# A snapshot copy moved on ScalarE, relu and square of the MLP moved to VectorE, and the last pair of a group split by unit, in a two-layer streaming encoder on one core

## The chip, the cores and the metric

One Trainium2 chip, one of its cores. A time is the device time in microseconds (us) of the whole kernel, one launch. The core has five engines that run their own instruction streams and meet at semaphores: TensorE (PE, with its weight loads shown as PEld), VectorE (DVE), ScalarE (ACT), GpSimd (POOL) and SyncE (SP, which issues the DMAs).

## The reference

Two layers over 512 prompt frames and 32 sample frames, which the kernel handles together as 544 columns. Each layer has a normalised projection, retention, gated linear attention and band attention in parallel, an output projection, and an MLP. The change is in the MLP:

```python
def channel_mix(h, n2, w_up_l, w_down_l):
    u = rmsnorm(h, n2) @ w_up_l                              # 1024 -> 4096
    return (jnp.square(jax.nn.relu(u)) @ w_down_l).astype(h.dtype)   # 4096 -> 1024
...
    for l in range(DEPTH):                                   # DEPTH = 2
        hp = hp + merge_heads(...)
        hp = hp + channel_mix(hp, norm2_w[l], w_up[l], w_down[l])
```

The RMS factor of the norm is not applied ahead of the up projection; the kernel scales after the down projection with its square (r2), which relu and square allow.

## The kernel before

All matrix products are made in fp32 with three passes: every operand is split into a high part (fp32r, a rounded copy made by ScalarE) and a rest (made by VectorE, original minus high part), and TensorE multiplies high by high, high by rest and rest by high. So each weight block and each activation passes through ScalarE (`whi`, `zhi`, ...) and then VectorE (`wlo`, `zlo`, ...) before TensorE can take it.

The MLP of a layer has four groups of 1024 hidden units (`GROUPS`). A group has eight units of 128 hidden rows, taken two at a time as four **pairs**, and then eight down units (`down` to `down + 7`). A pair is not multiplied out as it stands, but with seven products of quarter matrices (a fast scheme of the Strassen kind), numbered 6, 7, 5, 1, 2, 3, 4; each is 12 matmuls of 128x128 by 272 columns. TensorE's order in the steady state is `product(6, j)`, `(7, j)`, `(5, j)`, then `(1, j+1)`, `(2, j+1)`, then `(3, j)`, `(4, j)`. For the last pair of a group the first down unit stands between products 5, 3 and 4. The four weight combinations of a pair are `whi[0]/wlo[0]` (r0, also product 1 of the next pair), `R1h/R1l` (r1, products 6 and 7), `whi[1]/wlo[1]` (r2, product 5 and others) and `R3h/R3l` (r3, product 4).

Products accumulate in PSUM in part over each other, so ScalarE takes snapshots between them: `snap_s1` (L795 to L801) copies product 1 out of its bank before product 6 may add to it, `snap_u2` copies after product 6, before product 5, and `snap_x` after product 5. VectorE then adds snapshots and PSUM into the four quarters of `cb`, the pair's two units of 544 columns: `add_c11`, `add_c22`, `add_c21`; ScalarE writes c12 (`read_c12`). `post` (L828) on ScalarE then does relu in place, square in place and the high copy `zhi`, each over both units (1088 columns), and `rest_z` (L1503) on VectorE makes `zlo`. Down units wait for `z_lo` of the pair whose rows they use.

The order on every engine is written out by hand, in program order. Engines are in-order, so an instruction that waits holds all behind it. What matters here:
- At the MLP's start TensorE runs products 1 and 2 of the first pair (three quarters of 2, then 6 in part). `open_pair` (L1996) makes product 6 wait for `r1_lo` and `s1_read`, product 5 for `r2_lo` and `u2_read`, product 1 of the next pair for `r0_lo`.
- ScalarE at that point finishes the new activations of the MLP: `new_x` (L729) for the eighth tile, `hi_r2(0)`, `new_square(7)`, and then the loop over groups begins with `snap_s1(0)` (L906).
- VectorE in a pair: `add_c21(j-1)`, `lo_r2(j)`, `add_c11(j)`, `lo_r0(j+1)` (for the last pair `rest(down)`), `lo_r3(j)`, the sums of weights of the next pair, `add_c22(j)`, `rest_z(j-1)`, `lo_r1(j+1)`.
- After a group's last pair, in the first group of a layer only, VectorE works out r2 (an affine step and two reciprocals, L1583 and L1588), then in each group `rest(down+2)` and `scaled(0)` (L1526), which reads the first down unit out of PSUM. TensorE's `begin(down+2)` waits for both.
- GpSimd sums the squares and reduces them over partitions once a layer at the MLP's start, and adds each scaled down unit to `h`.

Of the kernel before, what the change touches and what calls it, by code (L numbers as in the profile page):

```python
# [9 lines left out]
KC = D // P  # L10
# [82 lines left out]
for _steps in (DVE_STEPS, ACT_STEPS):  # L93
# [16 lines left out]
    pvs_dve=4, gate_act=8, gate_dve=8, cat_dve=4, cat_hi=4, cat_lo=4, z_hi=16, z_lo=16,  # L110
# [59 lines left out]
def dve_x(name, kc):  # L170
    return len(DVE_X) * kc + DVE_X[name]

# [25 lines left out]
def hybrid_encoder(nc, x, wu, w_low, a2, small, bias, bias_s, st_ret, st_gla, ck, cv,  # L198
# [3 lines left out]
    with ctx:  # L202
# [115 lines left out]
        def sem(name):  # L318
# [25 lines left out]
            "split_act", "split_dve",  # L344
# [8 lines left out]
        with nc.Block() as block:  # L353
# [168 lines left out]
            def _(act):  # L522
# [10 lines left out]
                for layer in range(L):  # L533
# [192 lines left out]
                    def new_x(m):  # L726
# [13 lines left out]
                        else:  # L740
                            nc.scalar.activation(Xh[:, 1:3, kc, :], h[:, t, :].rearrange("p (a b) -> p a b", a=2), ACT.Copy,
                                                 scale=w).then_inc(sems["split_act"], 1)
                            act.wait_ge(sems["split_dve"], nth("split_dve", dve_x("t4_sum", kc)))
# [75 lines left out]
                    def read_c12(j):  # L819
# [3 lines left out]
                        if pair >= 2:  # L823
                            act.wait_ge(sems["z_lo"], pair - 1)
# [3 lines left out]
                    def post(j):  # L828

                        pair, q = up(j)[0], j % QUADS  # L830
                        act.wait_ge(sems["c12"], pair + 1)
                        act.wait_ge(sems["c21"], pair + 1)
                        link(nc.scalar.activation(cb[j % 2][:, :, :], cb[j % 2][:, :, :], ACT.Relu))
                        link(nc.scalar.activation(cb[j % 2][:, :, :], cb[j % 2][:, :, :], ACT.Square))
                        nc.scalar.activation(zhi[:, 2 * q:2 * q + 2, :], cb[j % 2][:, :, :], ACT.Copy).then_inc(sems["z_hi"], 1)

                    def next_x(m):
# [5 lines left out]
                        act.wait_ge(sems["z_lo"], nth("z_lo", PAIRS))  # L843
# [3 lines left out]
                    def last_squares(m):  # L847

                        act.wait_ge(sems["sq_used"], nth("sq_used", GROUPS * KC + m + 1))
                        act.wait_ge(sems["z_lo"], nth("z_lo", PAIRS))  # L850
# [53 lines left out]
                    for g in range(GROUPS):  # L904
                        j0, down = QUADS * g, UP + g * N_MLP + KC
                        snap_s1(j0)  # L906
# [20 lines left out]
                        post(j0 + QUADS - 1)  # L927
# [33 lines left out]
            def _(dve):  # L961
# [7 lines left out]
                for layer in range(L):  # L969
# [506 lines left out]
                    def add_c11(j):  # L1476
# [6 lines left out]
                        else:  # L1483
                            dve.wait_ge(sems["z_lo"], pair - 1)
# [17 lines left out]

                    def rest_z(j):  # L1503

                        pair, q = up(j)[0], j % QUADS
                        dve.wait_ge(sems["z_hi"], pair + 1)
# [46 lines left out]
                    for g in range(GROUPS):  # L1553
                        j0, down = QUADS * g, UP + g * N_MLP + KC
                        for j in range(j0, j0 + QUADS):
                            more = j + 1 < j0 + QUADS
                            if j > j0:
                                add_c21(j - 1)
                                lo_r2(j)
                            add_c11(j)  # L1560
# [19 lines left out]
                        rest_z(j0 + QUADS - 1)  # L1580
# [64 lines left out]
            def _(pe):  # L1645
# [6 lines left out]
                for layer in range(L):  # L1652
# [568 lines left out]
```

## Time and profile before

| | |
|---|---|
| three runs | 1408.93, 1405.13, 1407.30 us; median 1407.3 us |
| profiled execution, its own time | 1408.74 us |
| its span, first to last instruction | 1407.0 us |
| mean granted TensorE clock | 0.985 of full |
| TensorE matmul busy | 1352.0 us (96%) |
| VectorE busy | 939.8 us (67%) |
| ScalarE busy | 650.6 us (46%) |
| GpSimd busy | 155.4 us (11%) |
| DMA | 127.83 MB, 91 GB/s on average |

An engine's busy share is an average over the span. Matmuls overlap in the pipeline: one is listed at 0.29 us, but one starts every 0.126 us at the full clock. A bracket at the end of a timeline row tells how long the engine sat idle before that instruction, and what released it as far as the trace shows; "issue" means that nothing in the trace was found.

### The profile page before, as it was taken

The numbers are of one execution on the slowest core, as the hardware profiler recorded it, in microseconds if no ns is written. First come the engines' busy times: TensorE is split into PE (matmuls) and PEld (weight loads), VectorE is DVE, ScalarE is ACT, GpSimd is POOL, SyncE is SP. The second block draws the span as 40 slices with busy tenths as digits, with TensorE's granted clock in tenths as the row PEclk, the third lists the DMA queues.
The fourth block names the chain that finished last, engine by engine and source line by source line (L and its number), as shares of the span: only waits on it lengthen the run. The fifth ranks groups of instructions, "written<-read, shape, count | busy, mean of one in ns | idle before, by whom it ended". The sixth has DMA issues, their size and how long they took to land. (4 is left out here: it accounts for less than half of the span.)

```text
span 1407.0 us, 28738 instructions
## 1 busy us (share of the span) xinstructions
PE 1352.0 (96%) x12206; PEld 1307.8 (93%) x12206; DVE 939.8 (67%) x1464; ACT 650.6 (46%) x1043; POOL 155.4 (11%) x107
## 2 busy tenths in 40 slices
PE   9999999999999999999999999999999999999996
PEld 8899889899999999999998999889999999999996
DVE  6797766787657366475758967767774664746734
ACT  4423656655526337255333236565562362542731
POOL 0100000021120120210302000001201102012012
PEclk9999999999999999999999999999999999999998
DMA  5213333222322223222221223432222232232211
GB/s 218 76 57 109 96 111 103 76 90 75 104 92 77 91 90 105 81 85 93 91 75 47 67 84 119 132 97 76 76 75 98 84 106 90 76 105 90 87 64 64
DMA packets 50639, 127.83 MB, mean 91 GB/s; under 512 B 8400, under 2 KB 17744, under 8 KB 50512
## 3 DMA queue, kind: packets, MB, share of 16 engines
q1 hardware_dynamic: 50224, 125.44, 27.0%
q8 instruction: 97, 1.59, 0.5%
q10 hardware_dynamic: 288, 0.55, 0.1%
q14 instruction: 30, 0.25, 0.1%
HBM read 118.77 MB, written 7.21 MB: 90 GB/s over the span
## 5 line engine op out<-in xcount | busy, mean ns | idle before, releaser
L1666 PE MATMUL PS<-zhi,whi 128*128 128x272 f32 x1280 | 370.9, 290 | 15.4 <-DVE sq L1531 14.9
L1666 PE MATMUL PS<-zhi,wlo 128*128 128x272 f32 x1280 | 371.5, 290 | 0.0
L1666 PE MATMUL PS<-zlo,whi 128*128 128x272 f32 x1280 | 369.5, 289 | 0.0
L979 DVE TENSOR_TENSOR wlo<-raw,whi 128x1024 fp32r<-128x1024 f32 x136 | 169.0, 1243 | 162.4 <-ACT whi L548 161.5
L548 ACT ACTIVATE whi<-raw 128x1024 fp32r<-128x1024 f32 x136 | 143.4, 1056 | 286.8 <-PE PS L1666 281.3
L1666 PE MATMUL PS<-xhi,whi 128*128 128x272 f32 x896 | 270.2, 302 | 5.4 <-DVE xlo L984 2.9
L1666 PE MATMUL PS<-xhi,wlo 128*128 128x272 f32 x896 | 260.2, 290 | 0.0
L1666 PE MATMUL PS<-xlo,whi 128*128 128x272 f32 x896 | 259.5, 290 | 0.0
L1666 PEld LDWEIGHTS PS<-zhi,whi 128*128 128x128 f32 x1280 | 242.3, 189 | 17.4 <-DVE wlo L979 17.4
L1666 PEld LDWEIGHTS PS<-zlo,whi 128*128 128x128 f32 x1280 | 242.5, 189 | 0.0
L1666 PEld LDWEIGHTS PS<-zhi,wlo 128*128 128x128 f32 x1280 | 241.9, 189 | 0.0
L1666 PEld LDWEIGHTS PS<-xhi,whi 128*128 128x128 f32 x896 | 170.3, 190 | 17.1 <-issue 8.4
L1666 PEld LDWEIGHTS PS<-xlo,whi 128*128 128x128 f32 x896 | 170.6, 190 | 0.2
L513 POOL TENSOR_TENSOR h<-h,sq 128x544 f32<-128x544 f32 x62 | 102.1, 1650 | 620.8 <-DVE sq L1531 620.8
L1666 PEld LDWEIGHTS PS<-xhi,wlo 128*128 128x128 f32 x896 | 170.2, 190 | 0.0
L1666 PE MATMUL PS<-Xh,wlo 128*128 128x272 f32 x384 | 111.5, 290 | 0.0
L1666 PE MATMUL PS<-Xh,whi 128*128 128x272 f32 x384 | 111.4, 290 | 0.0
L1666 PE MATMUL PS<-Xl,whi 128*128 128x272 f32 x384 | 110.7, 288 | 0.0
L1666 PE MATMUL PS<-Th,R1h 128*128 128x272 f32 x256 | 76.5, 299 | 6.1 <-issue 6.1
L1666 PE MATMUL PS<-Th,R1l 128*128 128x272 f32 x256 | 76.1, 297 | 0.0
L1666 PE MATMUL PS<-Tl,R1h 128*128 128x272 f32 x256 | 75.7, 296 | 0.0
L1666 PEld LDWEIGHTS PS<-Xl,whi 128*128 128x128 f32 x384 | 72.8, 189 | 0.0
(282 smaller groups left out, 2445.7 us busy)
## 6 DMA issues: line engine op xcount, KB each, us to landing
raw<-in_wu SPq DMA_DIRECT2D x199, 512.0 KB, 3.5
Bh<-in_bias SPq DMA_DIRECT2D x16, 256.0 KB, 4.2
h<-in_x SPq DMA_DIRECT2D x8, 272.0 KB, 6.6
out_k_t<-att_k SPq DMA_DIRECT2D x8, 272.0 KB, 4.4
out_y_t<-y SPq DMA_DIRECT2D x8, 272.0 KB, 2.7
kct<-in_ck SPq DMA_DIRECT2D x8, 256.0 KB, 3.3
cvb<-in_cv SPq DMA_DIRECT2D x8, 256.0 KB, 3.9
out_v_p<-vtk SPq DMA_DIRECT2D x8, 256.0 KB, 2.2
```

The lines of the kernel that those rows point to most:

```text
L513: nc.gpsimd.tensor_tensor(h[:, m, :], h[:, m, :], sq[m % 2][:, :], ALU.add) \
L548: nc.scalar.activation(whi[n % SPL][:, :], raw[n % RAW][:, :], ACT.Copy).then_inc(sems["w_hi"], 1)
L979: nc.vector.tensor_tensor(wlo[n % SPL][:, :], raw[n % RAW][:, :], f32(whi[n % SPL][:, :]), ALU.subtract).then_inc(sems["w_lo"], 1)
L1666: return nc.tensor.matmul(out, lhsT, rhs, start=start, stop=stop, skip_group_check=True)
```

## The change

1. `snap_s1(0)`, the copy of product 1 of the layer's first pair, is issued inside `new_x` for the last tile, behind the high copy `Xh` and ahead of the copy `Th`, and no longer at the head of the first group. Other groups keep it where it was.
2. `post` on ScalarE keeps the high copy alone. Relu and square of a pair are one operation on VectorE, `relu_square`: `scalar_tensor_tensor` computes max(c, 0) * c over 1088 columns, in place. It stands between `lo_r2(j)` and `add_c11(j)`, for pair `j-1`. A new semaphore `row_squared` tells ScalarE.
3. The last pair of a group is split by its two units. Unit 0 (c11 and c12) stays on ScalarE (relu, square, high copy, 544 columns each); unit 1 gets its max-and-multiply on VectorE, its high copy on ScalarE; two rests of 544 columns on VectorE. Down products 6 and 7 wait each for their own unit. The counts of `z_hi` and `z_lo` go from 16 to 20 a layer.

TensorE's stream of instructions is the same in both kernels.

```diff
@@ new_x, last tile, ScalarE
                             nc.scalar.activation(Xh[:, 1:3, kc, :], h[:, t, :].rearrange("p (a b) -> p a b", a=2), ACT.Copy,
                                                  scale=w).then_inc(sems["split_act"], 1)
+                            if m == KC - 1:
+                                snap_s1(0)
                             act.wait_ge(sems["split_dve"], nth("split_dve", dve_x("t4_sum", kc)))
...
@@ ScalarE
                     def post(j):
                         pair, q = up(j)[0], j % QUADS
+                        act.wait_ge(sems["row_squared"], pair + 1)
+                        nc.scalar.activation(zhi[:, 2 * q:2 * q + 2, :], cb[j % 2][:, :, :], ACT.Copy).then_inc(sems["z_hi"], 1)
+
+                    def last_post(j):
+                        pair, c = up(j)[0], cb[j % 2]
+                        act.wait_ge(sems["c11"], pair + 1)
                         act.wait_ge(sems["c12"], pair + 1)
-                        act.wait_ge(sems["c21"], pair + 1)
-                        link(nc.scalar.activation(cb[j % 2][:, :, :], cb[j % 2][:, :, :], ACT.Relu))
-                        link(nc.scalar.activation(cb[j % 2][:, :, :], cb[j % 2][:, :, :], ACT.Square))
-                        nc.scalar.activation(zhi[:, 2 * q:2 * q + 2, :], cb[j % 2][:, :, :], ACT.Copy).then_inc(sems["z_hi"], 1)
+                        link(nc.scalar.activation(c[:, 0, :], c[:, 0, :], ACT.Relu))
+                        link(nc.scalar.activation(c[:, 0, :], c[:, 0, :], ACT.Square))
+                        nc.scalar.activation(zhi[:, KC - 2, :], c[:, 0, :], ACT.Copy).then_inc(sems["z_hi"], 1)
+                        act.wait_ge(sems["row_squared"], pair + 1)
+                        nc.scalar.activation(zhi[:, KC - 1, :], c[:, 1, :], ACT.Copy).then_inc(sems["z_hi"], 1)
...
@@ group loop, ScalarE
-                        snap_s1(j0)
+                        if g:
+                            snap_s1(j0)
...
-                        post(j0 + QUADS - 1)
+                        last_post(j0 + QUADS - 1)
...
@@ VectorE
+                    def relu_square(j):
+                        pair, c = up(j)[0], cb[j % 2]
+                        dve.wait_ge(sems["c12"], pair + 1)
+                        dve.wait_ge(sems["c21"], pair + 1)
+                        nc.vector.scalar_tensor_tensor(c[:, :, :], c[:, :, :], 0.0, c[:, :, :], ALU.max, ALU.mult) \
+                            .then_inc(sems["row_squared"], 1)
...
+                    def last_rest_z(j):
+                        pair, c = up(j)[0], cb[j % 2]
+                        dve.wait_ge(sems["c21"], pair + 1)
+                        nc.vector.scalar_tensor_tensor(c[:, 1, :], c[:, 1, :], 0.0, c[:, 1, :], ALU.max, ALU.mult) \
+                            .then_inc(sems["row_squared"], 1)
+                        for row in range(2):
+                            k = KC - 2 + row
+                            dve.wait_ge(sems["z_hi"], z_done(pair, row))
+                            nc.vector.tensor_tensor(zlo[:, k, :], c[:, row, :], f32(zhi[:, k, :]), ALU.subtract) \
+                                .then_inc(sems["z_lo"], 1)
...
@@ pair loop, VectorE
                                 add_c21(j - 1)
                                 lo_r2(j)
+                                relu_square(j - 1)
                             add_c11(j)
...
@@ down units, TensorE
-                            pe.wait_ge(sems["z_lo"], nth("z_lo", j0 + kc // 2 + 1))
+                            pe.wait_ge(sems["z_lo"], z_done(layer * PAIRS + j0 + kc // 2, kc % 2))
```

What the engines' streams look like at three places, before and then changed. First ScalarE at the start of the first layer's MLP. `Xh` and `Th` are high parts of activations, `whi1` is the weight high part r2 for product 5, `sq1` a square for the norm, `s1_sb` the snapshot of product 1, `whi0` the weight part r0 of the next pair, `u2_sb0` the snapshot that product 5 waits for.

```order
L741 ACTIVATE Xh_153<-h_57,sm_81 128x2x272 [waits unit_read]
L744 ACTIVATE Th_151<-tt1_164 128x3x272 [waits split_dve]
L783 ACTIVATE whi1_54<-Sx_159 128x1024 [waits unit_done,s4_ready]
L750 ACTIVATE sq1_65<-h_57 128x544 [waits sq_used]
L800 ACTIVATE s1_sb_165<-PS 128x272 [waits prod]
L765 ACTIVATE whi0_53<-raw2_51 128x1024 [waits prod,w_in2]
L808 ACTIVATE u2_sb0_167<-PS 128x272 [waits prod]
```

```order
L747 ACTIVATE Xh_153<-h_57,sm_81 128x2x272 [waits unit_read]
L808 ACTIVATE s1_sb_165<-PS 128x272 [waits prod]
L752 ACTIVATE Th_151<-tt1_164 128x3x272 [waits split_dve]
L791 ACTIVATE whi1_54<-Sx_159 128x1024 [waits unit_done,s4_ready]
L758 ACTIVATE sq1_65<-h_57 128x544 [waits sq_used]
L773 ACTIVATE whi0_53<-raw2_51 128x1024 [waits prod,w_in2]
L816 ACTIVATE u2_sb0_167<-PS 128x272 [waits prod]
```

`s1_sb` went from behind three instructions to ahead of them; the copy `whi0` and the snapshot `u2_sb0` follow `sq1` directly now.

Second VectorE in the middle of a group, pair 2 of the first group: `wlo1` is the rest for product 5, `cb` the pair's result, `wlo0` the rest for product 1 of the next pair.

```order
L1500 TENSOR_TENSOR cb1_161<-PS,u2_sb1_168 128x272 [waits u2_read,prod]
L1437 TENSOR_TENSOR wlo1_56<-Sx_159,whi1_54 128x1024 [waits r2_hi]
L1485 TENSOR_TENSOR cb0_160<-PS,s1_sb_165 128x272 [waits z_lo,s1_read,prod]
L1437 TENSOR_TENSOR wlo0_55<-raw2_51,whi0_53 128x1024 [waits r0_hi]
L1437 TENSOR_TENSOR R3l_158<-raw1_50,R3h_157 128x512 [waits r3_hi]
L1459 TENSOR_TENSOR Sx_159<-raw3_52 128x512 [waits r1_lo,r2_lo,w_in3,w_in2]
```

```order
L1517 TENSOR_TENSOR cb1_161<-PS,u2_sb1_168 128x272 [waits u2_read,prod]
L1454 TENSOR_TENSOR wlo1_56<-Sx_159,whi1_54 128x1024 [waits r2_hi]
L1525 SCALAR_TENSOR_TENSOR cb1_161<-cb1_161 128x1088 [waits c21,c12]
L1502 TENSOR_TENSOR cb0_160<-PS,s1_sb_165 128x272 [waits z_lo,s1_read,prod]
L1454 TENSOR_TENSOR wlo0_55<-raw2_51,whi0_53 128x1024 [waits r0_hi]
L1454 TENSOR_TENSOR R3l_158<-raw1_50,R3h_157 128x512 [waits r3_hi]
L1476 TENSOR_TENSOR Sx_159<-raw3_52 128x512 [waits r1_lo,r2_lo,w_in3,w_in2]
```

One more operation of 1088 columns stands ahead of `wlo0`, `R3l` and all behind them. In the last pair of a group `wlo0` at this place is the rest of the first down unit.

Third VectorE behind the last pair of the first group: `zlo` is the pair's rest, `r2` the scale of the down units, `wlo0` the rest of the third down unit, `sq0` the read of the first one.

```order
L1500 TENSOR_TENSOR cb1_161<-PS,u2_sb1_168 128x272 [waits u2_read,prod]
L1507 TENSOR_TENSOR zlo_61<-cb1_161,zhi_60 128x1088 [waits z_hi]
L1583 TENSOR_SCALAR r2_63<-rstd_62 128x544 [waits ss_all]
L1588 RECIPROCAL r2_63<-r2_63 128x272 [waits r2_steps] x2
L979 TENSOR_TENSOR wlo0_55<-raw2_51,whi0_53 128x1024 [waits w_hi,r2_steps]
L1531 TENSOR_TENSOR sq0_64<-PS,r2_63 128x544 [waits sq_used,unit_done]
```

```order
L1517 TENSOR_TENSOR cb1_161<-PS,u2_sb1_168 128x272 [waits u2_read,prod]
L1539 SCALAR_TENSOR_TENSOR cb1_161<-cb1_161 128x544 [waits c21]
L1544 TENSOR_TENSOR zlo_61<-cb1_161,zhi_60 128x544 [waits z_hi] x2
L1621 TENSOR_SCALAR r2_63<-rstd_62 128x544 [waits ss_all]
L1626 RECIPROCAL r2_63<-r2_63 128x272 [waits r2_steps] x2
L996 TENSOR_TENSOR wlo0_55<-raw2_51,whi0_53 128x1024 [waits w_hi,r2_steps]
L1568 TENSOR_TENSOR sq0_64<-PS,r2_63 128x544 [waits sq_used,unit_done]
```

The rest of 1088 columns became a max-and-multiply and two rests, 544 columns each; what stands behind keeps its order.

## Rows read from the trace of the kernel before

**Rows 1.** Waits of TensorE, whole span: us in total, times, longest.
```profile
PE PS L1666 <- DVE sq L1531: 14.9, 8, 2.4
PE PS L1666 <- issue: 6.1, 2, 3.0
```

**Rows 2.** TensorE's timeline: start us, us, engine, line, operation, [idle before].
```profile
321.90 0.29 PE L1666 MATMUL PS<-Xh,wlo 128*128 128x272 f32 x1
325.23 0.56 PE L1666 MATMUL PS<-Th,R1h 128*128 128x272 f32 x1 [3.04 <-issue]
...
331.54 0.36 PE L1666 MATMUL PS<-Th,whi 128*128 128x272 f32 x1
```

**Rows 3.** ScalarE's timeline at the start of the first layer's MLP.
```profile
320.47 0.75 ACT L741 ACTIVATE Xh<-h,sm 128x544 fp32r<-128x544 f32 x1 [0.59 <-DVE h L1383]
...
324.21 0.64 ACT L750 ACTIVATE sq<-h 128x544 f32<-128x544 f32 x1
324.76 0.38 ACT L800 ACTIVATE s_sb<-PS 128x272 f32<-128x272 f32 x1
328.38 1.06 ACT L765 ACTIVATE whi<-raw 128x1024 fp32r<-128x1024 f32 x1 [3.25 <-PE PS L1666]
331.05 0.40 ACT L808 ACTIVATE u_sb<-PS 128x272 f32<-128x272 f32 x1 [1.60 <-PE PS L1666]
```

**Rows 4.** Stretches: us, busy (instructions) PE, PEld, DVE, ACT, POOL; granted clock; DMA.
```profile
324.50:331.20 6.70, 5.97 (x26) 6.00 (x27) 3.23 (x4) 1.85 (x4) 1.83 (x1) 0.50 0.00 0
...
382.50:385.80 3.30, 3.16 (x14) 3.19 (x15) 1.76 (x2) 0.00 (x0) 3.21 (x2) 0.50 0.65 185
```

**Rows 5.** VectorE's timeline in pair 2 of the first group.
```profile
350.00 0.44 DVE L1500 TENSOR_TENSOR cb<-PS,u_sb 128x272 f32<-128x272 f32 x1 [1.71 <-PE PS L1666]
...
351.84 1.21 DVE L1437 TENSOR_TENSOR wlo<-raw,whi 128x1024 fp32r<-128x1024 f32 x1
...
356.48 1.28 DVE L1507 TENSOR_TENSOR zlo<-cb,zhi 128x1088 fp32r<-128x1088 f32 x1
357.68 1.22 DVE L1437 TENSOR_TENSOR R1l<-Sx,R1h 128x1024 fp32r<-128x1024 f32 x1
360.61 0.44 DVE L1500 TENSOR_TENSOR cb<-PS,u_sb 128x272 f32<-128x272 f32 x1 [1.71 <-PE PS L1666]
```

**Rows 6.** TensorE's weight loads, the first one of product 1 of pair 3.
```profile
354.22 0.19 PEld L1666 LDWEIGHTS PS<-Xh,whi 128*128 128x128 f32 x1
```

**Rows 7.** VectorE, TensorE and its weight load at the second group's third down unit.
```profile
475.84 0.71 DVE L1531 TENSOR_TENSOR sq<-PS,r 128x544 f32<-128x544 f32 x1
...
476.67 0.19 PEld L1666 LDWEIGHTS PS<-zhi,whi 128*128 128x128 f32 x1 [1.88 <-DVE wlo L979]
476.70 0.36 PE L1666 MATMUL PS<-zhi,whi 128*128 128x272 f32 x1 [1.68 <-DVE sq L1531]
```

**Rows 8.** VectorE by form: count, busy us, mean ns, idle before.
```profile
L1351 DVE TENSOR_TENSOR G<-G,sq 128x544 f32<-128x544 f32 x8 | 5.8, 725 | 1.4 <-DVE G L1345 0.5 <-ACT sq L868 0.4
...
L1342 DVE SCALAR_TENSOR_TENSOR sq<-G,sq 128x544 f32<-128x544 f32 x8 | 5.8, 722 | 3.1 <-ACT sq L864 3.1
```

**Rows 9.** GpSimd's reduction at the start of the MLP.
```profile
332.51 3.43 POOL L507 PARTITION_ALL_REDUCE rstd<-ssum  x1 [5.75 <-issue]
```

**Rows 10.** VectorE beside that reduction.
```profile
334.12 1.32 DVE L1473 TENSOR_TENSOR Sx<-raw,Sx 128x512 f32<-128x512 f32 x1
```

**Rows 11.** End of the first group, ScalarE.
```profile
368.48 1.05 ACT L548 ACTIVATE whi<-raw 128x1024 fp32r<-128x1024 f32 x1
```

**Rows 12.** End of the first group, VectorE.
```profile
371.21 0.44 DVE L1500 TENSOR_TENSOR cb<-PS,u_sb 128x272 f32<-128x272 f32 x1 [0.42 <-PE PS L1666]
375.18 1.29 DVE L1507 TENSOR_TENSOR zlo<-cb,zhi 128x1088 fp32r<-128x1088 f32 x1 [3.53 <-ACT zhi L835]
...
380.64 1.22 DVE L979 TENSOR_TENSOR wlo<-raw,whi 128x1024 fp32r<-128x1024 f32 x1
```

**Rows 13.** End of the first group, TensorE.
```profile
382.64 0.56 PE L1666 MATMUL PS<-zhi,whi 128*128 128x272 f32 x1 [2.42 <-DVE sq L1531]
```

More of the change, by code:

```diff
@@ L109 @@
     norm_s=4, pe_turn=8, turned=24, pe_turn_s=4, turned_s=4, pe_pv=4, pv_act=4, pv_dve=4, pe_pv_s=4, pvs_act=4,
-    pvs_dve=4, gate_act=8, gate_dve=8, cat_dve=4, cat_hi=4, cat_lo=4, z_hi=16, z_lo=16,
+    pvs_dve=4, gate_act=8, gate_dve=8, cat_dve=4, cat_hi=4, cat_lo=4, z_hi=20, z_lo=20,
     split_act=20, split_dve=32,
@@ L171, in dve_x, with z_done @@
     return len(DVE_X) * kc + DVE_X[name]
+def z_done(pair, row=1):
+    group, q = divmod(pair, QUADS)
+    return (QUADS + 1) * group + q + (1 if q < QUADS - 1 else 1 + row)
 BANK_A, BANK_B, BANK_C = (4, 5), (2, 6), (3, 7)
@@ L343, in hybrid_encoder @@
             "gate_act", "gate_dve", "cat_dve", "cat_hi", "cat_lo", "z_hi", "z_lo", "out_dma", "stored0", "stored1", "dve_link", "act_link",
-            "split_act", "split_dve",
+            "split_act", "split_dve", "row_squared",
             "s_steps", "s4_ready", "r0_hi", "r0_lo", "r1_hi", "r1_lo", "r2_hi", "r2_lo", "r3_hi", "r3_lo", "prod",
@@ L823, in read_c12 @@
                         if pair >= 2:
-                            act.wait_ge(sems["z_lo"], pair - 1)
+                            act.wait_ge(sems["z_lo"], z_done(pair - 2))
                         nc.scalar.activation(cb[j % 2][:, 0, HT:T], PS[:, BANK_A[j % 2], 0:HT], ACT.Copy) \
@@ L842, in next_x @@
                             act.wait_ge(last_added, 2 * (layer + 1))
-                        act.wait_ge(sems["z_lo"], nth("z_lo", PAIRS))
+                        act.wait_ge(sems["z_lo"], nth("z_lo", z_done(PAIRS - 1)))
                         xhi_tile(m, w0 + NSM)
@@ L849, in last_squares @@
                         act.wait_ge(sems["sq_used"], nth("sq_used", GROUPS * KC + m + 1))
-                        act.wait_ge(sems["z_lo"], nth("z_lo", PAIRS))
+                        act.wait_ge(sems["z_lo"], nth("z_lo", z_done(PAIRS - 1)))
                         squares(m, L)
@@ L1483, in add_c11 @@
                         else:
-                            dve.wait_ge(sems["z_lo"], pair - 1)
+                            dve.wait_ge(sems["z_lo"], z_done(pair - 2))
                         nc.vector.tensor_tensor(cb[j % 2][:, 0, 0:HT], PS[:, BANK_C[j % 2], 0:HT], s1_sb[:, :], ALU.add) \
@@ L1501, in add_c21 @@
                             .then_inc(sems["c21"], 1)
+                    def relu_square(j):
[4 more added lines that the diff above has]
+                            .then_inc(sems["row_squared"], 1)
                     def rest_z(j):
                         pair, q = up(j)[0], j % QUADS
-                        dve.wait_ge(sems["z_hi"], pair + 1)
+                        dve.wait_ge(sems["z_hi"], z_done(pair))
                         nc.vector.tensor_tensor(zlo[:, 2 * q:2 * q + 2, :], cb[j % 2][:, :, :], f32(zhi[:, 2 * q:2 * q + 2, :]),
                                                 ALU.subtract).then_inc(sems["z_lo"], 1)
+                    def last_rest_z(j):
[8 more added lines that the diff above has]
+                                .then_inc(sems["z_lo"], 1)
                     for m in range(1, KC + 1):
@@ L1579, in _ @@
                         add_c21(j0 + QUADS - 1)
-                        rest_z(j0 + QUADS - 1)
+                        last_rest_z(j0 + QUADS - 1)
                         if g == 0:
```

## The prediction

> **What bounds the kernel now.** The first view is the page: TensorE is busy for 96% of the span, VectorE for 67% and ScalarE for 46%. So only what stops TensorE, or halves its clock, can move the time, and work taken off ScalarE is worth nothing by itself. The second view is the list of TensorE's waits [rows 1]. Two entries lie in the MLP: two waits of 3.0 us that end with "issue", and eight waits, 14.9 us together, before a down unit. The third view is the timeline around them.
>
> The two of 3.0 us are the start of each layer's MLP. TensorE starts the last matmul of product 2 at 321.90 and the first of product 6 at 325.23 [rows 2]. Product 6 adds into the bank that holds product 1 and waits for `s1_read`; the snapshot starts on ScalarE at 324.76 and takes 0.38 us [rows 3], so the wait ends 0.09 us behind it. The copy is last in a queue: nothing it needs was missing since product 1 ended. The fourth view, busy time by stretch, shows what follows: from 324.5 to 331.2 the clock is at 0.50, the lower of its two levels (1.2 of 2.4 GHz), and 26 matmuls go through in 6.7 us [rows 4]. At the full clock a pair of 84 matmuls takes 10.61 us [rows 5], 0.126 us each.
>
> The eight others are one at each group's end: the third down unit waits for its weight rest and for the read of the first. Two are 2.42 us and the other six 1.68: 4.84 and 10.08 make the 14.9 [rows 1, 7, 13]. The two are the first group of each layer, where two reciprocals stand in VectorE's queue behind the pair's rest. Behind 2.42 the clock falls to 0.50 for 3.3 us [rows 4].
>
> **The snapshot moved.** The last of the nine matmuls of product 2 that are run first starts at 321.90 [rows 2] and makes way 0.126 us later, at 322.03; product 1 ended nine matmuls earlier, at about 320.9, and its end is seen some 0.2 us later. ScalarE is in `Xh` until 321.22 [rows 3]. The snapshot then runs to about 321.6, before TensorE asks at 322.03. `Th` behind it waits for VectorE and starts at 322.47 as now, so the copy hides in idle time. If that cover were gone it would cost 0.38 us a layer.
>
> What is late next? Between 322.03 and product 5 stand 27 matmuls, 3.4 us at the full clock: 325.43. Product 5 waits for `u2_read`. ScalarE frees at 324.76, where the snapshot stood; then the copy of the next pair's weights, 1.06 us, then `u2`, 0.40 us [rows 3]: product 5 can start at about 326.25. Now it starts at 331.54 [rows 2]. The wait of 3.04 becomes one of 0.8, and I expect no fall of the clock from that: behind a wait of 1.68 the first matmul takes 0.36 us, behind one of 2.42, at half clock, 0.56 [rows 7, 13]. Gain 5.29 us a layer, **-10.6 us**, of which 2.2 a layer is the wait and about 3.1 the clock.
>
> **Relu and square on VectorE.** The operation is not in the trace at this size. `scalar_tensor_tensor` with two fp32 inputs in SBUF and a fixed scalar takes 722 ns for 544 columns, `tensor_tensor` 725 [rows 8]; `zlo`, 1088 columns of `tensor_tensor`, takes 1.28 us, and the next starts 1.20 us after it [rows 5]. Bounds: 0.72 us below, if 1088 columns cost what 544 do, and 2.4 above, if the operation cost double per column (1.28 us and twice the 0.56 that 544 more columns cost). I take 1.20, by the row of the same kind of operation. VectorE idles 1.71 us in each pair [rows 5], so it fits: 0.5 us stay.
>
> But it stands ahead of `wlo0`, which product 1 of the next pair needs. That rest runs from 351.84 to 353.05 [rows 5]; with 1.20 in front it ends at 354.25. TensorE loads the first weights of product 1 at 354.22 [rows 6], and a load follows the end of what released it by 0.12 us (475.84 + 0.71 to 476.67 [rows 7]). So the load comes at 354.37 and TensorE loses 0.15 us. In a group's last pair the first down unit stands at the same place. Three pairs of a group have the operation ahead of them, four groups, two layers: 24 times 0.15, **+3.6 us**; 0 if the latency is already covered, 6 at 0.25 each. The rest for product 6, `R1l`, ends at 358.90 now [rows 5] and at 360.1 then; TensorE begins product 6 some 0.2 us before VectorE's next sum at 360.61 [rows 5], so it is late only if the operation is 0.3 us longer than I think. The 2.2 us a pair that ScalarE is rid of hide beside TensorE: 0.
>
> Eight rows of this kind of operation say 722 against 725 ns [rows 8]. The Trainium skill, Vector Engine (DVE) Microarchitecture Reference, section "Points that are easy to get wrong", says that this instruction with two SBUF sources wider than bf16 runs at half throughput. By that rule the time would be that of the third rival below; the trace does not agree with it.
>
> **Beside GpSimd.** The reduction starts at 332.51 and takes 3.43 us [rows 9]; a VectorE operation of 512 columns beside it took 1.32 us [rows 10], where 544 columns take 0.73 elsewhere [rows 8]. The first pair comes 5.3 us earlier now while the reduction does not, so `lo_r2` or `relu_square` falls into it: VectorE slips 0.6 us where it has no slack, **+1.2 us** for both layers, and 0.2 each for `wlo0` of pair 1 beside the last addition of squares, **+0.4**. Bounds 0 and 3.4.
>
> The Trainium skill, SBUF — State Buffer, section "SBUF: two separate sides", says that VectorE with two SBUF inputs and GpSimd exclude each other from the shared ports for an instruction's whole length. By it the sum would have up to 1.5 us a layer here in place of 0.6. Rows 9 and 10 agree that they get in each other's way, but with 0.6.
>
> **The last pair split.** Now the pair's last sum starts at 371.21 and its rest ends at 376.47 [rows 12]. Then: sum, 0.36; max-and-multiply of unit 1, 0.72 [rows 8]; its high copy on ScalarE about 0.65; its rest 0.72: about 373.8. Unit 0 runs on ScalarE from 369.5, where the weight copy ends [rows 11], three steps of about 0.65, and is ready by 371.6. In groups behind the first, TensorE does not wait for this rest now either, so there it gains nothing. In the first group r2 is ready 2.6 us earlier: from the rest's end to the next weight rest is 4.17 us [rows 12], so at 378.0, ahead of the weight copy that waits for TensorE. The wait becomes that of the other groups: 2.42 - 1.68 = 0.74 a layer, **-1.5 us**. And 3.3 us at half clock are no more, half of each regained, **-3.3 us**. Bounds for both together: 0 and -5.
>
> **The sum**, against the profiled execution: 1408.7 - 10.6 + 3.6 + 1.6 - 1.5 - 3.3 = 1398.5, a change of -10.2 us. That execution is 1.4 us over the median of the three runs, so against the median 1407.3 the forecast is **1397.1 us**. A run tells 0.3% (4.2 us) from no change.
>
> **Rivals.**
> Nothing lost in the pairs: TensorE's loads are asked for early enough, and the 3.6 and 1.6 us vanish. For it: the 0.15 is smaller than the spread of how I read the latency. Against it: one weight load follows the other without a gap [rows 6]. 1407.3 - 15.4 = 1391.9 us.
> The clock stays low: the waits shrink, but the clock at the MLP's start or the first group's end falls all the same, since 0.8 us of waiting are left and stalls of pairs come on top. For it: it fell behind a wait of 2.42 [rows 4, 13]. Against: it did not behind 1.68 [rows 7]. With both places low, 3.1 twice and 3.3 come back: 1406.6; with one of them, 1400.4 or 1403.3.
> VectorE becomes the bound: the operation at 2.4 us, 1.1 longer, makes `wlo0` 1.3 us late in each of 24 places, +30 in place of +3.6: 1424 us, slower. It is what the page's rule above would bring. It decides from 1.20 + 0.45 us on, where 24 stalls of 0.58 us eat up the 13.8 gained. Against it are rows 8.
> The snapshot is no help: it is early, yet product 6 waits for another that comes as late. The rests for product 6's first three quarters were made tiles ago, and the last quarter's is asked for 2.6 us after 322.03, so little speaks for it. 1397.1 + 10.6 = 1407.7 us.
>
> **Chances.** Forecast as worked out 0.54, nothing lost in the pairs 0.22, clock low 0.13 (half of it within 0.3%), snapshot no help 0.05, VectorE the bound 0.06. Faster by over 0.3%: 0.54 + 0.22 + 0.07 = 0.83; within 0.3% 0.11; slower 0.06. The range goes from the second case, 1 us less for the luck of where the clock falls elsewhere, to the clock case with one place low: 1391 to 1402.5.
>
> **What would show it.** In the changed profile: `s_sb` about 0.1 us behind `Xh`, and no TensorE wait of 3.0 but one near 0.8 before product 5, or none; clock 1.00 there. The new operation at 1.28 us, and small idle times of PEld, 0.1 to 0.2, at product 1 and the first down unit, released by `wlo`; `R1l` never the releaser. Eight waits at group ends, all near 1.7. The forecast is wrong if the operation takes over 1.5 us, if the clock is at 0.50 at one of the four places, or if the wait at the start is over 1.5 us.

## The result and the profile after

The median went from 1407.3 us (5 runs, 1403.98 to 1408.93) to **1398.93 us** (5 runs, 1398.03 to 1400.52). The ratio, with its 95% interval, is 0.9946 (0.9928 to 0.9964): a small gain, but clear of the noise. The forecast was 1397.1 us, with a range of 1391 to 1402.5. The profiled execution took 1398.03 us (span 1395.6, mean granted clock 0.990), against 1408.74 (1407.0, 0.985) before.

First the span and the busy times of the page of the changed kernel, then its list of TensorE's waits (total us, times, longest):

```profile
span 1395.6 us, 28738 instructions
PE 1347.3 (97%) x12206; PEld 1301.8 (93%) x12206; DVE 975.1 (70%) x1504; ACT 595.4 (43%) x1003; POOL 155.4 (11%) x107
```

```profile
PE PS L1704 <- DVE sq L1568: 13.9, 8, 2.0
```

The entry that ended with "issue", two waits of 3.0 us [rows 1], is gone. The eight waits before a down unit are still there, 13.9 us instead of 14.9, and the longest is 2.0, not 1.7 as forecast. TensorE's timeline has the places (start, us, operation, idle time before it):

```profile
320.40 0.29 PE L1704 MATMUL PS<-Xh,wlo 128*128 128x272 f32 x1
320.53 0.29 PE L1704 MATMUL PS<-Th,R1h 128*128 128x272 f32 x1
...
324.68 0.36 PE L1704 MATMUL PS<-Th,whi 128*128 128x272 f32 x1 [0.47 <-issue]
...
375.58 0.36 PE L1704 MATMUL PS<-zhi,whi 128*128 128x272 f32 x1 [1.75 <-DVE sq L1568]
...
655.98 0.36 PE L1704 MATMUL PS<-zhi,whi 128*128 128x272 f32 x1 [1.98 <-DVE sq L1568]
```

Product 6 follows product 2 without a gap, where 3.04 us stood [rows 2]; product 5 starts 4.28 us behind that last matmul of product 2, where it took 9.64. The last two rows are two group ends, the first and the last of layer 0. ScalarE's timeline shows why:

```profile
318.97 0.75 ACT L747 ACTIVATE Xh<-h,sm 128x544 fp32r<-128x544 f32 x1 [0.59 <-DVE h L1400]
319.63 0.38 ACT L808 ACTIVATE s_sb<-PS 128x272 f32<-128x272 f32 x1
320.98 0.89 ACT L752 ACTIVATE Th<-tt 128x816 fp32r<-128x816 f32 x1 [0.97 <-DVE tt L1435]
321.77 1.05 ACT L791 ACTIVATE whi<-Sx 128x1024 fp32r<-128x1024 f32 x1
322.72 0.64 ACT L758 ACTIVATE sq<-h 128x544 f32<-128x544 f32 x1
323.26 1.04 ACT L773 ACTIVATE whi<-raw 128x1024 fp32r<-128x1024 f32 x1
324.21 0.37 ACT L816 ACTIVATE u_sb<-PS 128x272 f32<-128x272 f32 x1
```

The snapshot `s_sb` starts right behind `Xh` and is over at 320.01, before TensorE asks at 320.53; `Th` still waits for VectorE. Product 5 starts 0.10 us behind the end of `u_sb`: that copy is the next to come late. The clock at four places (stretch and length, then busy time and count of PE, PEld, DVE, ACT and POOL, granted clock, DMA share and GB/s):

```profile
320.50:324.50 4.00, 3.71 (x29) 3.39 (x27) 3.74 (x7) 3.52 (x5) 1.06 (x1) 1.00 0.18 74
324.70:331.30 6.60, 6.60 (x50) 6.40 (x51) 5.73 (x7) 1.80 (x4) 1.00 (x2) 1.00 0.15 32
376.70:380.00 3.30, 3.30 (x17) 3.30 (x16) 0.50 (x1) 0.00 (x0) 2.38 (x2) 0.50 0.79 251
656.60:660.00 3.40, 3.40 (x17) 3.40 (x17) 0.43 (x1) 2.24 (x3) 0.66 (x1) 0.50 0.34 131
```

It stays full at the start of the MLP, where it was 0.50 for 6.7 us [rows 4]. It still falls behind the first group of layer 0, and now behind that layer's last group too. In layer 1 neither happens.

With the span divided at the starts of the same matmuls, the difference lies here (us; worked out from the two timelines):

```
stage                                         before   after   difference
start to last matmul of product 2's piece     321.90   320.40    -1.50
to product 5 (snapshot)                         9.64     4.28    -5.36
to the third down unit of group 0              51.10    50.90    -0.20
three more groups, layer 0                    279.39   280.40    +1.01
to layer 1's last matmul of product 2's piece 349.55   349.67    +0.13
to product 5, layer 1                           9.65     4.29    -5.37
to the third down unit of group 0              51.10    51.25    +0.15
three more groups, layer 1                    279.30   278.65    -0.65
to the end                                     55.37    55.76    +0.39
                                                        sum     -11.4
```

The first line isn't the change's: up to the snapshot itself no instruction differs. Before, the clock was low for 6.8 us from 10.4 on; after, it was low for only 3.4 us, from 52.4 on.

VectorE in one pair of the changed kernel, the new operation in the middle:

```profile
343.46 0.44 DVE L1517 TENSOR_TENSOR cb<-PS,u_sb 128x272 f32<-128x272 f32 x1 [0.61 <-PE PS L1704]
343.82 1.22 DVE L1454 TENSOR_TENSOR wlo<-Sx,whi 128x1024 fp32r<-128x1024 f32 x1
344.95 1.28 DVE L1525 SCALAR_TENSOR_TENSOR cb<-cb 128x1088 f32<-128x1088 f32 x1
346.15 0.43 DVE L1502 TENSOR_TENSOR cb<-PS,s_sb 128x272 f32<-128x272 f32 x1
346.50 1.22 DVE L1454 TENSOR_TENSOR wlo<-raw,whi 128x1024 fp32r<-128x1024 f32 x1
...
354.14 0.44 DVE L1517 TENSOR_TENSOR cb<-PS,u_sb 128x272 f32<-128x272 f32 x1 [0.60 <-PE PS L1704]
```

It takes 1.20 us of the queue (344.95 to 346.15), and VectorE's idle time in a pair goes from 1.71 [rows 5] to 0.60. `wlo` ends at 347.72; the first weights of product 1 follow in the loads' timeline:

```profile
347.56 0.19 PEld L1704 LDWEIGHTS PS<-Th,wlo 128*128 128x128 f32 x1
347.77 0.19 PEld L1704 LDWEIGHTS PS<-Xh,whi 128*128 128x128 f32 x1
```

That load was due 0.13 behind the one before, at 347.69, and is 0.08 late. The pair takes 10.68 us instead of 10.61, a group 92.88 instead of 92.66, which is three times 0.07.

### The profile page after: what moved, and what is told of

Its sections match the earlier page's. It is cut to its first block and busy times, and to the rows that moved or that the text cites. A ratio compares the mean times of both kernels' runs of the same rounds, so it can differ in the third digit from the quotient of the medians.

```text
span 1395.6 us, 28738 instructions
## 1 busy us (share of the span) xinstructions
PE 1347.3 (97%) x12206; PEld 1301.8 (93%) x12206; DVE 975.1 (70%) x1504; ACT 595.4 (43%) x1003; POOL 155.4 (11%) x107
## 5 line engine op out<-in xcount | busy, mean ns | idle before, releaser
L1704 PE MATMUL PS<-zhi,whi 128*128 128x272 f32 x1280 | 371.5, 290 | 14.3 <-DVE sq L1568 13.9
L1704 PEld LDWEIGHTS PS<-Xh,whi 128*128 128x128 f32 x384 | 72.2, 188 | 1.4 <-DVE wlo L1454 0.8
```

The lines of the kernel that those rows point to most:

```text
L1704: return nc.tensor.matmul(out, lhsT, rhs, start=start, stop=stop, skip_group_check=True)
```

## The experiments

Each ratio is against the kernel before on the same chip, with its 95% interval; it need not be the quotient of the two medians. The kernel before had a median of 1404.9 us in the series of e1 to e4, 1404.5 in that of e5 to e10, and 1405.8 in that of e11 to e14.

**e1, the snapshot alone**, in the kernel before:

```diff
@@ xt, behind Xh
+                            if m == KC - 1:
+                                snap_s1(0)
@@ mlp
-                        snap_s1(j0)
+                        if g:
+                            snap_s1(j0)
```

> The kernel before with only the snapshot of the layer's first product moved between Xh and Th; relu, square and high copy stay on ScalarE, the last pair is not split. Theory (each part adds up, the snapshot is worth the wait and the clock behind it): product 5 of the first pair comes 5.3 to 5.4 us earlier in each layer, no half clock at the MLP's start, -10.7 us against before, 1396.6. Rival (the snapshot's gain is the wait alone, the clock that is gained comes back elsewhere): -4.4 to -6, 1402. Rival (the snapshot is the whole of the measured change, and the other parts are worth nothing): -8.4.

Measured: 1399.61 us, ratio 0.9954 (0.9939 to 0.9968): 6.5 us less by the ratio, 5.3 by the medians. In its profile the wait of 3.04 is gone in both layers, the clock is full there, and product 5 comes 4.28 us behind product 2's last matmul, 5.36 and 5.37 earlier; the first groups still end with 2.42 and a low clock. So the mechanism holds alone, but the times show less than 10.7 us. The rival, that the clock's gain comes back elsewhere, has one thing for it: in this profile the clock is low for 6.8 us from 694.6 on, at a wait of 2.95 us between the layers, and that costs some 1.5 us which the profile before doesn't have. But it isn't the snapshot's doing: the kernel before has such a fall at the same place in its second profile (e10), and e9, e12 and e13, with the snapshot moved, have none.

**e2, the changed kernel without the snapshot:** the same edit taken back.

> The changed kernel with the snapshot back at the head of the first group; relu_square on VectorE and the split last pair stay. Theory: the wait of 3.0 us and the half clock behind it are back in each layer; pairs cost 0.07 us in 24 places (+1.8), the first group's end gives 1.3 to 1.5 and up to 3.3 of clock: 1404 to 1407, within 0.3% of before. Rival (VectorE's operation costs the 0.15 us a place of the prediction): 1406 to 1409.

Measured: 1405.32 us, 0.9998 (0.9988 to 1.0008). Without the snapshot no net gain is left: what the split brings (e3) and what the squares cost cancel. The wait of 3.04 is back in both layers. The clock behind it is low for 6.8 us in layer 0, where the windows show 26 matmuls in 5.8 us, and for 3.4 us in layer 1:

```profile
323.80:329.60 5.80, 5.80 (x26) 5.80 (x27) 2.33 (x4) 1.11 (x2) 1.47 (x1) 0.50 0.00 0
```

**e3, the split of the last pair alone**; the other pairs and the snapshot as before:

```diff
@@ post (ScalarE), the first three pairs of a group
+                        link(nc.scalar.activation(cb[j % 2][:, :, :], cb[j % 2][:, :, :], ACT.Relu))
+                        link(nc.scalar.activation(cb[j % 2][:, :, :], cb[j % 2][:, :, :], ACT.Square))
@@ VectorE's order
                                 lo_r2(j)
-                                relu_square(j - 1)
```

> The kernel before with only the last pair of each group split by unit; the other pairs keep relu, square and high copy on ScalarE, the snapshot stays where it was. Theory: the r2 chain starts 2.6 us earlier, the third down unit of the first group of each layer waits 1.7 instead of 2.4 us (-1.4 in all), and the clock behind it is low in none, one or two of the layers (-3.3, -1.7 or 0): 1402.6 to 1406. No change in the periods of the other groups (92.66 us). Rival (a wait of 1.7 never lowers the clock): 1402.6 in every run.

Measured: 1401.76 us, 0.9981 (0.9966 to 0.9995). The first groups' waits went from 2.42 to 1.75, without a fall behind them. And the MLP's start showed what I had not expected; here are TensorE's timeline and the windows:

```profile
324.55 0.36 PE L1703 MATMUL PS<-Th,R1h 128*128 128x272 f32 x1 [3.05 <-issue]
...
328.33 0.36 PE L1703 MATMUL PS<-Th,whi 128*128 128x272 f32 x1 [0.15 <-issue]
```

```profile
324.60:328.00 3.40, 3.40 (x27) 3.36 (x27) 1.25 (x3) 1.22 (x2) 1.50 (x1) 1.00 0.00 0
1011.20:1014.60 3.40, 3.40 (x27) 3.26 (x27) 1.24 (x3) 1.32 (x2) 1.39 (x1) 1.00 0.00 0
```

The same wait of 3.05, in both layers, and the clock stays full: 27 matmuls in 3.4 us. Nothing in this kernel that runs ahead of 324.55 differs from the kernel before. Its twelve executions fall into two groups, seven of 1400.2 to 1402.1 us and five of 1404.3 to 1406.9 with a lower mean clock; the profile is of one of the seven. Product 5 comes here 7.1 us behind product 2's last matmul (3.05 + 3.78 and the 0.3 of that matmul); with the moved snapshot it is 4.28. So the wait alone is worth 2.8 us a layer, and only with the clock's fall of 6.8 us is it 5.36.

**e4, relu_square behind the rests:** in the changed kernel the operation stands behind `wlo` instead of ahead of it.

```diff
                                 lo_r2(j)
-                                relu_square(j - 1)
                             add_c11(j)
...
                             if j > j0:
+                                relu_square(j - 1)
                                 lo_r3(j)
```

> The changed kernel with relu_square of the pair before moved behind lo_r0 (in a group's last pair behind the first down unit's rest). Theory (the 0.07 us a place are its position ahead of wlo0): the groups' periods go from 92.88 back to 92.66 us, -1.8 us against the changed kernel, 1397.1. Rival (the period is longer because VectorE works beside something else, a port or a bank): period stays 92.88. Rival (what now comes later, the high copy and the snapshot behind it on ScalarE, is late for product 3): periods above 92.9.

Measured: 1395.93 us, 0.993 (0.9917 to 0.9944). The group takes 92.64 us (468.36 to 561.00), as before the change: the 0.22 a group was the operation ahead of the rest. The last group of layer 0 still waits 1.96 with a low clock behind it. A second run, e11:

> The kernel with the late relu_square again, now on the same chip as the one without it. Theory (relu_square on VectorE is worth nothing to TensorE; both have periods of 92.66 us and the rest is where the clock falls): within 2 us of the kernel without it. Rival (relu_square also brings something that costs, as the last group's wait of 1.97 in layer 0 in place of 1.68 and the low clock behind it, seen in all five kernels that have it): 1.5 to 2.5 us slower than without it, and that wait and low clock again.

Measured: 1396.05 us, 0.9935 (0.9922 to 0.9949), with the same wait (1.96) and fall.

**e5, a longer operation:** in the changed kernel `relu_square` gets a second operation of 544 columns that changes no value.

```diff
-                        nc.vector.scalar_tensor_tensor(c[:, :, :], ..., ALU.max, ALU.mult) \
+                        link(nc.vector.scalar_tensor_tensor(c[:, :, :], ..., ALU.max, ALU.mult))
+                        nc.vector.scalar_tensor_tensor(c[:, 0, :], c[:, 0, :], 0.0, c[:, 0, :], ALU.max, ALU.max) \
                             .then_inc(sems["row_squared"], 1)
```

> The changed kernel with VectorE's work per pair made longer: relu_square is followed, behind a link, by max(c, c) over 544 columns, which changes no value; about 0.7 us more ahead of wlo0 in each of 24 pairs. Theory (a place costs what wlo0 is late, beyond its slack): 0.07 becomes 0.77 us, groups' periods go from 92.88 to about 95.0 us, +17 us against the changed kernel, 1416. Rival (TensorE has some other slack at product 1 and hides part): below +8. Rival (VectorE becomes the bound of the whole pair): more than 1.2 us a place, over +28.

Measured: 1414.7 us, 1.0061 (1.0041 to 1.0081). VectorE's and TensorE's timelines in one pair:

```profile
347.07 1.29 DVE L1525 SCALAR_TENSOR_TENSOR cb<-cb 128x1088 f32<-128x1088 f32 x1
348.39 0.72 DVE L1526 SCALAR_TENSOR_TENSOR cb<-cb 128x544 f32<-128x544 f32 x1
349.03 0.43 DVE L1502 TENSOR_TENSOR cb<-PS,s_sb 128x272 f32<-128x272 f32 x1
349.38 1.22 DVE L1454 TENSOR_TENSOR wlo<-raw,whi 128x1024 fp32r<-128x1024 f32 x1
```

```profile
350.65 0.39 PE L1705 MATMUL PS<-Xh,whi 128*128 128x272 f32 x1 [0.57 <-DVE wlo L1454]
```

`wlo` ends at 350.60, and TensorE, load and matmul, starts 0.05 behind it. What is added ahead of `wlo` comes out of TensorE in full: the group takes 95.11 us, 95.0 were expected. The changed kernel stands just past the edge of its slack, with 0.07 a pair.

**e8, the first scaled rest ahead of the second weight rest** at the group's end, on top of e4:

```diff
                         for m in range(1, KC):
+                            if m == 1:
+                                scaled(0, g)
```

> As the run with the late relu_square (1395.9), and scaled(0), the read of the first down unit, stands ahead of rest(down + 2) on VectorE. Theory (the wait at each group's end is the chain split, rest, read, and the read need not stand behind the rest): the wait goes from 1.68 to about 1.05 us in eight places, -5.1 us, 1390.8. Rival (GpSimd's addition starts 2.2 us earlier and stands in the way of the rest, which has two inputs in SBUF): the rest takes 2 us in place of 1.22 and nothing is gained, 1396.

Measured: 1397.47 us, 0.994 (0.9925 to 0.9954), no gain over e4. The waits are 1.88 in the first groups, where e4 has 1.75 and 1.76, and 1.80 or 1.81 in the others, where it has 1.68 or 1.69 (1.96 in the last group of layer 0). Three of the eight are followed by a low clock. VectorE, and then GpSimd, at one group's end:

```profile
467.29 2.07 DVE L996 TENSOR_TENSOR wlo<-raw,whi 128x1024 fp32r<-128x1024 f32 x1 [0.43 <-ACT whi L554]
```

```profile
466.94 1.34 POOL L519 TENSOR_TENSOR h<-h,sq 128x544 f32<-128x544 f32 x1 [51.65 <-DVE sq L1568]
```

The read of the first down unit, moved forward, lets GpSimd's addition start earlier, beside the weight rest that TensorE waits for, and that rest takes 2.07 us instead of 1.22. That is the rival that was named.

**e9, the snapshot and the split without the squares on VectorE:** the changed kernel with the first three pairs of each group done on ScalarE, as in e3's diff.

> The changed kernel without relu_square in the first three pairs of a group (ScalarE does relu and square of them as before); snapshot moved and last pair split. Theory (relu_square buys TensorE nothing, it costs 0.07 us a place): same as with the late relu_square, 1395.9, groups' periods 92.66. Rival (ScalarE, freed of relu and square, gives TensorE something): 1397.5 or more.

Measured: 1394.01 us, 0.9915 (0.99 to 0.9929), the fastest of all. Its list of waits:

```profile
PE PS L1706 <- DVE sq L1571: 13.6, 8, 1.8
```

Groups of 92.66 us, a wait of 1.69 in the last group of layer 0, and no low clock in either MLP; the span is 1391.3 us, the mean clock 0.994. The same kernel was run again as e12:

> The kernel with the snapshot moved and the last pair split, no relu_square in the other pairs, on the same chip. Theory: 1394, 0.990 to 0.993 of before, no wait over 1.76 us in the MLPs and no low clock there.

Measured: 1395.11 us, 0.9934 (0.9918 to 0.995), the same waits and again no low clock in the MLPs.

**e10, the kernel before, profiled once more:**

> The kernel before, unchanged, profiled a second time. Theory (whether the clock falls behind a wait depends on where the wait lies against something that runs free of the kernel): the waits are the same as in the first profile (3.04, 2.42, 1.68 us), but the stretches of low clock behind them are not all at the same places. Rival (a wait of 3 us always lowers the clock): both MLP starts show 6.8 us of half clock again, both first groups' ends 3.4.

Measured: 1409.03 us, one execution. The wait of 3.04 (3.05 here) is there in both layers, but in layer 0 the clock was low for 3.4 us behind it, half as long as [rows 4]; product 5 came 5.16 us behind product 6, where it took 6.31 [rows 2]. In layer 1 it was low for 6.8 us again. The two windows of layer 0:

```profile
324.50:328.00 3.50, 3.03 (x13) 3.06 (x14) 0.80 (x1) 0.37 (x2) 1.83 (x1) 0.52 0.00 0
328.00:331.40 3.40, 3.25 (x26) 3.05 (x25) 2.63 (x4) 1.46 (x2) 0.00 (x0) 0.99 0.00 0
```

**e13 and e14, other places for the snapshot**, in the kernel before: behind `Th` of the last tile, and ahead of the loop over groups, behind the copy for r2.

```diff
                             nc.scalar.activation(Th[:, 1:4, kc, :], ...)
+                            if m == KC - 1:
+                                snap_s1(0)        # e13
...
+                    snap_s1(0)                    # e14
                     for g in range(GROUPS):
```

> The kernel before with the snapshot behind Th, one place later than in the change. The first wait becomes about 1.5 us in place of 3.04. Theory (the clock falls behind long waits only; none fell behind 1.68, two of twelve behind 1.75, all behind 1.97 and 2.42): no low clock at the MLP's start, product 5 about 5.1 us behind the last matmul of product 2 (4.3 with the snapshot at its new place), total 1 to 2 us over the snapshot alone. Rival (any wait there lowers the clock): product 5 at 8 us.

Measured: 1400.92 us, 0.9967 (0.9952 to 0.9981): waits of 1.54 and 1.57, and no fall of the clock behind them. Product 5 comes 5.62 and 5.65 us behind product 2's last matmul; 5.1 was expected.

> The kernel before with the snapshot behind hi_r2(0), ahead of the square. The first wait becomes about 2.5 us. Theory: the clock falls in at least one of the two layers, and product 5 comes 6.5 to 9 us behind product 2; total 0 to 3 us under before. Rival (a wait of 2.5 is short enough): product 5 at 6.0 in both layers, no low clock.

Measured: 1404.59 us, 0.9992 (0.9979 to 1.0006): waits of 2.50 in both layers. The same stretch in the two layers:

```profile
324.40:327.60 3.20, 3.20 (x14) 3.20 (x15) 0.98 (x2) 0.49 (x2) 1.56 (x1) 0.50 0.00 0
1011.20:1014.40 3.20, 3.20 (x26) 3.20 (x27) 1.58 (x3) 1.42 (x3) 1.57 (x1) 1.00 0.00 0
```

One wait is followed by half clock and 14 matmuls, the other by full clock and 26.

## Why the prediction came out

The forecast was -10.2 us against the profiled execution. The two profiled executions stand 10.7 apart (their spans 11.4), of which 1.5 is the low clock at the program's start; the medians stand 8.4 apart. By its own steps:

**The snapshot, -10.6: right in these two profiles** (-10.73), and right in why. Product 5 was to come 4.35 us behind product 2's last matmul and came 4.28. Counted as the forecast counts it, 28 starts of 0.126 us behind 320.40, the wait there is 0.75; the row has 0.47, mostly because it counts from the end of the matmul before. The shares were off: the forecast gave 2.2 us a layer to the wait and 3.1 to the clock, and with the clock full behind the same wait (e3) they are 2.84 and 2.52. What was wrong is that I took the clock's part as certain. It is part of the gain only in executions in which the clock falls: e3 shows it not falling behind 3.05, e10 and e2 show it falling for half as long in one layer. So both layers together are worth between 5.7 and 10.7 us in one execution. Over many executions it is 6.5 us by e1's ratio, and 7.3 if e2's ratio is set against the changed kernel's. The chance of a low clock stood in the text for the kernel after alone; the kernel before needed one too.

**The squares in pairs, +3.6: right place, half the size.** 24 places times 0.07 are +1.7. The number that was off is the latency of 0.12 us from the end of the rest to the load. I had it from another wait [rows 7]; here it is 0.05 (347.72 to 347.77; in e5 350.60 to 350.65). With it the forecast's own working gives 354.30 against 354.22, 0.08. e4 takes the term away and e5 raises it as expected, so the mechanism is shown.

**The size of the new operation: right.** The operation groups of VectorE in the changed kernel (busy us, mean ns; idle before):

```profile
L1525 DVE SCALAR_TENSOR_TENSOR cb<-cb 128x1088 f32<-128x1088 f32 x24 | 30.8, 1285 | 0.0
L1532 DVE TENSOR_TENSOR zlo<-cb,zhi 128x1088 fp32r<-128x1088 f32 x24 | 30.8, 1284 | 0.0
```

1285 against 1284 ns, so the rival of an operation at 2.4 us is out. The Trainium skill's rule of half throughput (Vector Engine (DVE) Microarchitecture Reference, "Points that are easy to get wrong") doesn't hold for this operation, measured against `tensor_tensor` of the same size.

**Beside GpSimd, +1.6: right in kind, about half the size.** The addition of squares was to cost 0.2 a layer. The first pair's `wlo` did fall beside it (2.02 us at 324.34), and TensorE's load for product 1 waited 0.20 us for it. The runs with the moved snapshot and no squares on VectorE show this term alone: from product 5 to the third down unit the first groups take 51.34 us in e1 against 51.10 before, and 50.65 to 50.68 in e9 and e12 against 50.43 in e3. That is 0.24 a layer, +0.5. The reduction was to cost 0.6 a layer. In layer 0 it cost nothing: the only rest beside it (333.13) took its usual 1.22. In layer 1 the rest for product 5 came earlier in the reduction and took 1.60, and the load for product 1 behind it waited 0.41 us:

```profile
1016.52 3.43 POOL L513 PARTITION_ALL_REDUCE rstd<-ssum  x1 [5.99 <-issue]
```

```profile
1018.39 1.60 DVE L1454 TENSOR_TENSOR wlo<-Sx,whi 128x1024 fp32r<-128x1024 f32 x1
```

```profile
1022.72 0.19 PEld L1704 LDWEIGHTS PS<-Xh,whi 128*128 128x128 f32 x1 [0.41 <-DVE wlo L1454]
```

That is 0.37 more than the 0.24 and the usual 0.07 a pair. In e1 and e12 the same rest is stretched as well (1.51 and 1.73 in layer 1) and nothing is lost, for without the squares VectorE has time to make it up. Both together: +0.9.

**The split, -1.5 for the waits: nearly** (1.75 each, -1.3, alone in e3). **-3.3 for the clock: a third of it.** The clock fell behind 1.75 in layer 0 and not in layer 1; it fell behind neither in e3, e9 and e12. And a fall costs less than the 1.65 us it was priced at. Before, the groups behind the two falls took 94.06 and 93.97 us in place of 92.66, so 2.7 us were there to be gained; now the group behind the one fall takes 94.38 in place of 92.88. That leaves -1.2. One of the prediction's own signs of being wrong has come, the clock at 0.50 at one of the four places, and on this term the forecast failed. The step that failed is that a wait of 1.7 was taken as safe, from six waits of 1.68: over all runs 1.68 is, and 1.75 is not quite.

**Not forecast: the wait of 1.98 in the last group of layer 0** (1.68 before). It is 1.96 to 1.98 in every kernel with the squares on VectorE but e8 (the changed kernel, e2, e4, e5, e11), and in none without; five times of five the clock fell behind it. But that fall costs nothing. Layer 1's first big wait, for `xlo`, shrinks by as much, as TensorE's timeline shows:

```profile
695.39 0.39 PE L1704 MATMUL PS<-xhi,whi 128*128 128x272 f32 x1 [1.45 <-DVE xlo L1001]
```

Before it was 2.93, and between the two matmuls lie 39.41 us now and 39.40 then. So only the 0.29 counts. The place of it can be told: the copy `whi`, which the third down unit's rest waits for, starts 0.3 us late on ScalarE.

```profile
652.89 1.06 ACT L554 ACTIVATE whi<-raw 128x1024 fp32r<-128x1024 f32 x1 [6.00 <-PE PS L1704]
```

In every other group of the kernels with the split the idle time ahead of this copy is 5.70 or 5.71 us. The semaphore events in the trace have TensorE's release at 652.51, so ScalarE starts 0.38 us behind it; in the other groups it is 0.08. e8 has this late start as well (0.36), though its wait is 1.81. Why ScalarE is late there, and only with the squares on VectorE, stays open.

The terms as measured: -10.7 + 1.7 + 0.9 - 1.3 - 1.2 = -10.6 in place of -10.2; with -1.5 at the program's start, +0.3 for the longer wait, +0.1 at the start of layer 1 and +0.4 at the end, that is the 11.4 of the span but for 0.1 of rounding. That the sum came so near is luck in part: 1.9 us too much for the squares and 0.7 too much beside GpSimd made up for 2.1 too much for the clock at the first groups' ends. And the medians, 8.4 us apart, hold less of the clock than the -10.6 of the snapshot has in it.

**What the squares buy: nothing.** e9 and e12 without them stand at 0.9915 and 0.9934, e4 and e11 with them behind the rest at 0.993 and 0.9935, the changed kernel at 0.9946. The 2.2 us a pair that ScalarE is rid of were hidden, as forecast. A version with the snapshot and the split alone is the best here: 0.3 and 0.1% under the changed kernel by its ratios. The intervals still overlap (e9's by 0.0001), and neither e9 nor e12 was timed in one series with the changed kernel, so that it is the best is likely, not shown.

## What to carry to other kernels

A copy that needs nothing new and yet is last in a queue is worth moving, and the queue's next late entry, not the wait removed, gives the gain. Where a wait is followed by a low clock in one execution, price it with the clock's part and without, and take a second profile of the kernel before. Before an operation is put ahead of a rest that the busiest engine waits for, look whether it fits behind: there it cost nothing in a pair, ahead of it 0.07 us, and the 0.7 us that e5 added counted in full.

## What the runs showed of the hardware

Whether TensorE's clock goes from its upper level (2.4 GHz) to the lower (1.2 GHz) behind a wait is not settled by the wait's length. Counted over the MLPs of all 14 profiles, by the wait in front: 1.54 to 1.69 us, no fall in 75; 1.75 and 1.76, 2 of 16; 1.80 to 1.88, 3 of 8; 1.96 to 1.98, 5 of 5; 2.42 to 2.50, 9 of 12; 3.04 and 3.05, 6 of 8. Between the layers, where TensorE waits 2.93 to 2.98 us for `xlo` in eight of the profiles, it is 3 of 8 (e1, e3, e10). The first matmul behind 3.05 us went either way in two kernels with the same code ahead of it (e10 and e3, layer 0), and behind 2.50 in the two layers of one execution (e14). What decides it between 1.75 and 3.05 isn't known from these runs.

A low clock can be free: the one at 656.6 us was made up in the next wait for VectorE (2.93 to 1.45).

What VectorE loses beside GpSimd depends on when it gets there. Rests of 1024 columns took 2.02 and 2.07 us beside an addition of 544 columns (spans of GpSimd are rough). They had started 0.94 and 0.99 us ahead of the addition's end and lost 0.80 and 0.85. Beside the reduction of 3.43 us the loss is set by how far the reduction has come. A rest that starts 2.25 us behind the reduction's start takes its usual 1.22 (333.13 and 330.88); at 1.87 it takes 1.60 (1018.39 and 1016.52); at 0.14, in e3, it takes 3.32:

```profile
331.76 3.32 DVE L1454 TENSOR_TENSOR R1l<-Sx,R1h 128x1024 fp32r<-128x1024 f32 x1 [0.17 <-ACT R1h L779]
```

All three end 3.46 or 3.47 us behind the reduction's start, and so do the other rests that start in its first 2.2 us, but for one in e14, where the reduction itself took 3.76. The 512 columns of [rows 10] fit in: 1.61 us behind the start, 1.32 in place of 0.69. So the reduction holds such an operation up to 2.25 us behind its own start, and from there on not at all. Where the rest starts first, 0.14 us ahead of the reduction (e3, layer 1), the rest takes 1.23 and the reduction 4.37.

The Trainium skill (SBUF — State Buffer, "SBUF: two separate sides") has VectorE with two SBUF inputs and a GpSimd operation that reads SBUF exclude each other, with whichever starts first holding the ports for the whole instruction. The additions in these runs come near to that (0.80 lost of 0.94), and so does who starts first in e3; for the reduction it holds for the first 2.25 us and not for the whole 3.43.
